# Six experts' weights in three pair slots, and the compressed cache pages spread 5, 7 and 4 a lane over both projections

## The reference

```python
past_cmp = cmp_pool[page_table].reshape(B, PAST_LEN, 2, NSA_KV_HEADS, NSA_HD)
m = kv_rows.astype(F32).reshape(B, L // CMP_BLOCK, CMP_BLOCK, 2, NSA_KV_HEADS, NSA_HD).mean(axis=2)
```

```python
w = jax.nn.softmax(top_l, axis=-1) * grp_w
eid = grp_i * EXPERTS_PER_GROUP + top_i
h = jax.nn.silu(jnp.einsum('nd,edf->nef', x2, w_gate)) * jnp.einsum('nd,edf->nef', x2, w_up)
y = jnp.einsum('nef,efd->nd', h * combine.astype(h.dtype)[..., None], w_down)
```

## Time and profile before

| | |
|---|---|
| median of three runs | 2153.87 us (2149.84 to 2154.89) |
| the profiled execution's own time | 2150.78 us |
| its span | 2149.0 us |
| PE busy | 1638.4 us (76%) |
| DVE busy | 790.3 us (37%) |
| ACT busy | 494.2 us (23%) |
| POOL busy | 181.0 us (8%) |
| queue q1, which carries SP's DMAs | 421.77 MB |
| mean granted clock of PE | 0.857 |

### The profile page before, as it was taken

The page is one execution under the profiler, slowest core; times in us unless marked ns, Lnnn a source line. Parts: engine busy times, 40 slices in busy tenths (PEclk is TensorE's granted clock), DMA queues, the critical chain, the costliest instruction groups (busy, mean ns, idle before and its releaser), DMA issues. The chain is left out here.

```text
span 2149.0 us, 35773 instructions
## 1 busy us (share of the span) xinstructions
PE 1638.4 (76%) x12824; PEld 1195.2 (56%) x12824; DVE 790.3 (37%) x1836; ACT 494.2 (23%) x1250; POOL 181.0 (8%) x282
## 2 busy tenths in 40 slices
PE   4999977888697487775898477875766687487875
PEld 3888866677486244444777355652433376354443
DVE  1666323556302211112155537665544302211112
ACT  2111751222102011111000046773111101111110
POOL 0000003112100311110000000000000000211110
PEclk8999977998597699987799768997787788699997
DMA  3555425200117399992499610006899526299995
GB/s 112 184 173 181 158 79 197 83 5 4 62 59 285 112 426 425 423 407 103 142 313 314 227 63 1 2 2 222 321 343 331 195 69 272 66 424 424 424 422 200
DMA packets 130596, 443.41 MB, mean 206 GB/s; under 512 B 22001, under 2 KB 27634, under 8 KB 112562
## 3 DMA queue, kind: packets, MB, share of 16 engines
q1 hardware_dynamic: 114274, 421.77, 51.7%
q0 software_dynamic: 11008, 17.89, 2.3%
q10 hardware_dynamic: 5200, 2.23, 0.4%
HBM read 426.35 MB, written 43.77 MB: 219 GB/s over the span
## 5 line engine op out<-in xcount | busy, mean ns | idle before, releaser
L1903 PE MATMUL moe_experts_bank_gu<-moe_weights_gu,moe_experts_xT 128*64 128x256 f32 x2048 | 258.4, 416 | 66.5 <-DMA moe_weights_gu<-in_w_gate_up 50.1
L1903 PEld LDWEIGHTS moe_experts_bank_gu<-moe_weights_gu,moe_experts_xT 128*64 128x64 f32 x2048 | 170.6, 151 | 165.8 <-issue 117.5
L408 PE MATMUL proj_acc<-h_gdn,proj_w 128*128 128x272 f32 x1024 | 238.0, 395 | 13.9 <-DMA proj_w<-in_gdn_w 13.9
L408 PEld LDWEIGHTS proj_acc<-h_gdn,proj_w 128*128 128x128 f32 x1024 | 195.8, 191 | 54.9 <-DMA proj_w<-in_gdn_w 14.3
L2143 PE MATMUL nproj_acc<-nsa_h,nproj_w 128*128 128x272 f32 x640 | 151.0, 396 | 11.2 <-DMA nproj_w<-in_nsa_w 11.2
L2143 PEld LDWEIGHTS nproj_acc<-nsa_h,nproj_w 128*128 128x128 f32 x640 | 120.8, 191 | 41.1 <-DMA nproj_w<-in_nsa_w 17.0
L1924 PE MATMUL moe_experts_bank_y<-moe_weights_down,moe_experts_hT 128*64 128x512 f32 x512 | 116.9, 598 | 25.8 <-ACT moe_experts_hT L1953 25.8
L1984 DVE SCALAR_TENSOR_TENSOR moe_experts_h<-moe_experts_bank_gu,moe_table,moe_experts_gate 128x128 f32<-128x128 f32 x64 | 22.5, 351 | 300.0 <-ACT moe_experts_gate L1948 300.0
L282 DVE TENSOR_REDUCE nsa_past_c<-nproj_raw 128x4096 f32 x20 | 88.4, 4420 | 113.2 <-DMA nproj_raw<-in_cmp_pool 113.2
L1656 POOL DMA_INDIRECT table<-moe_router_entry,moe_router_slot_of x20 | 19.2, 962 | 997.1 <-DVE moe_router_place L1614 991.6
L282 DVE TENSOR_REDUCE first_sums<-proj_raw 128x1536 f32 (+1 forms) x32 | 56.1, 1753 | 92.1 <-DMA proj_raw<-in_cmp_pool 92.1
(11 more groups left out here) (487 smaller groups left out, 2582.8 us busy)
## 6 DMA issues: line engine op xcount, KB each, us to landing
moe_weights_gu<-in_w_gate_up SPq DMA_DIRECT2D x64, 2048.0 KB, 20.9
moe_weights_down<-in_w_down SPq DMA_DIRECT2D x64, 1024.0 KB, 22.5
ring_kv<-in_slc_pool SPq DMA_DIRECT2D x256, 256.0 KB, 5.0
nproj_raw<-in_cmp_pool SPq DMA_DIRECT2D x160, 256.0 KB, 4.3
proj_raw<-in_cmp_pool SPq DMA_DIRECT2D x96, 256.0 KB, 2.8
proj_w<-in_gdn_w SPq DMA_DIRECT2D x32, 512.0 KB, 3.2
nproj_w<-in_nsa_w SPq DMA_DIRECT2D x20, 512.0 KB, 5.9
moe_results_y<-y_rows SPq DMA_DIRECT2D x16, 512.0 KB, 6.8
```

The lines of the kernel that those rows point to most:

```text
L408: mm = pe.matmul(acc[s][:, a, 0:HALF], w[s][:, k, :], g.hT[:, k, a * HALF:(a + 1) * HALF], start=(k == 0), stop=(k == KT - 1))
L1903: mm = pe.matmul(gu_bank[m][H, 0:FF], ln.xT[:, k, H], w.gu[:, k, m * FF:(m + 1) * FF], start=(k == 0), stop=(k == KT - 1))
```

## The change

Three things are changed.

*Experts.* `MOE_SLOTS` = 3 pair slots hold the weights of six experts; pair n uses slot n mod 3, while tokens, results and the two lanes stay as they were. `prefetch` loads all six. Thirteen pairs are loaded during the stage, each once the pair three before it has finished with the slot. The loop over pairs is unrolled on all engines, with the pair's number known.

*Room for them.* The expert's h is written over its gate (ACT's silu waits for the turn of h one round before), the norm's squares are written to the buffer that the normed tokens go to, the empty table is the table's own buffer, and the router's row buffers and turned tiles are halves: each token tile is turned, copied and stored as two halves of 512 columns, on buffer 0 and 1. A copy of a tile from 1 on now waits for the same half of the tile before to have landed.

*Pages.* GDN's projection sums 5 pages in each of the 24 convolution tiles and 7 in each of the 8 z tiles, NSA's 4 in each of its 20; `PAGES_EARLY` becomes 176. SP's loop over z tiles is unrolled.

```diff
+MOE_SLOTS = 3
-PAGES_GDN = 3
-PAGES_NSA = 8
-PAGES_EARLY = PAGES_GDN * (CONV_TILES + HEADS)
+PAGES_CONV, PAGES_Z, PAGES_NSA = 5, 7, 4
+PAGES_CONV_END = PAGES_CONV * CONV_TILES
+PAGES_EARLY = PAGES_CONV_END + PAGES_Z * HEADS
...
-        sq = st.sb("sq", [P, KT, TOKENS])
+        sq = g.hT
...
-                with sp.Fori(0, rounds + z_rounds - 1) as i:
+                with sp.Fori(0, rounds) as i:
                     for s in range(2):
...
+                        load_weights(s, i)
+                        pages.load(sp, s, i, (2 * i + s) * PAGES_CONV, PAGES_CONV)
+                for i in range(z_rounds):
+                    for s in range(2):
+                        if i < z_rounds - 1:
+                            load_weights(s, rounds + i)
+                        pages.load(sp, s, rounds + i, PAGES_CONV_END + (2 * i + s) * PAGES_Z, PAGES_Z)
...
-        empty = st.sb("empty", [P, TABLE_COLUMNS, WORDS], U32)
-        rows = [st.sb(f"rows{s}", [P, D_MODEL]) for s in range(2)]
+        empty = g.table
+        rows = [st.sb(f"rows{s}", [P, D_MODEL // 2]) for s in range(2)]
...
+                    for a in range(2):
+                        act.wait_ge(rows_turned, 2 * t + a + 1)
+                        if t >= 1:
+                            act.wait_ge(stored[a], 16 * t)
+                        act.activation(rows[a][0:n, :], turned[a][0:n, :], ACT.Copy).then_inc(rows_out, 1)
...
-            weights = [ExpertWeights(g, st, s, layer) for s in range(2 * MOE_LANES)]
+            weights = [ExpertWeights(g, st, s, layer) for s in range(2 * MOE_SLOTS)]
...
-            ln.h = st.sb(f"h{s}", [P, FF])
+            ln.h = ln.gate
...
-                with eng.Fori(0, rounds) as i:
-                    body(p * rounds + i, i)
+                for pair in range(PAIRS):
+                    body(lanes[pair % MOE_LANES], p * rounds + pair // MOE_LANES, p, pair)
...
-                with sp.Fori(0, rounds - 1) as i:
-                    for ln in lanes:
-                        load(ln, i, i + 1)
+                for pair in range(MOE_SLOTS, PAIRS):
+                    load(pair, (0, pair - MOE_SLOTS))
...
+                            act.wait_ge(ln.pe.sem, ln.pe.past(f"h turned {m}", r - 1))
```

More of the change, by code:

```diff
@@ L1755, in experts_stage @@
             ln.s = s
-            ln.w = weights[2 * s:2 * s + 2]
             ln.x = st.sb(f"x{s}", [P, D_MODEL])
@@ L1777, in over_experts, with weights_of, landed @@
             with eng.Fori(0, passes) as p:
-                with eng.Fori(0, rounds) as i:
-                    body(p * rounds + i, i)
-            return passes
+                for pair in range(PAIRS):
+                    body(lanes[pair % MOE_LANES], p * rounds + pair // MOE_LANES, p, pair)
+            return passes
+        def weights_of(pair):
+            slot = pair % MOE_SLOTS
+            return weights[2 * slot:2 * slot + 2]
+        def landed(p, pair):
+            return 16 * (p * slot_uses(pair % MOE_SLOTS) + pair // MOE_SLOTS + 1)
         def before(ln, r):
@@ L1811, in _ @@
                     with sp.Fori(1, passes) as p:
-                        with sp.Fori(0, rounds) as i:
-                            for ln in lanes:
-                                load(ln, p * rounds + i - 1, i)
+                        for pair in range(PAIRS):
+                            slot = pair % MOE_SLOTS
+                            last_of_slot = slot + MOE_SLOTS * (slot_uses(slot) - 1)
+                            load(pair, (p, pair - MOE_SLOTS) if pair >= MOE_SLOTS else (p - 1, last_of_slot))
             @block.gpsimd
```

244 lines of the change are left out of this document (119 added, 125 removed).

## The result

The changed kernel takes 2158.57 us (median of 20 runs) where the kernel before, in runs between them, takes 2152.2: a ratio of 1.0026, interval 1.0014 to 1.0037. It is slower, by 3 to 8 us, which the 20 runs of each tell from no change. The prediction had 2151, 3 us under the median of before that it started from. The 20 times lie in two bunches, eight from 2153.56 to 2155.9 and twelve from 2158.07 to 2164.14.

What follows compares the result with a forecast made beforehand. It took the experts as bound by DMA, GDN's projection by PE, NSA's by PE and its end by SP. -23.5 + 11 + 10 = -2.5 from the median 2153.87 gave 2151 us, own range 2143 to 2159, whole range 2130 to 2166.

Steps and rivals of the forecast that it cites:

- NSA: NSA's projection with four pages for eight: waits for weights go and its end shortens, -23.5 us (-21 to -26).
- GDN: GDN's projection with five and seven pages for three: z tiles make PE late, +11 us (+7 to +13).
- The tail: End of NSA's projection, last product to next stage: +12.7 us for +25.0, so 12.3 less.
- 1.8 of room: GDN z tile on ACT: the logarithm could wait 1.8 us; a multiplication 6.7 later makes it 4.9 late.
- The hold at the first z tile: GDN, behind the last convolution tile: its taps end later and make the first z product 2.3 us late.
- The tail behind the last product: End of GDN's projection: the seven pages' sum and the multiplications take 11.1 us where 6.7 stood.
- Experts: Third slot: 14.9 us less loading per layer against a router 20 later, +10 us for both layers (+8 to +24).
- the delay: Router: row stores behind the longer preload make PE's counts 20 us later per layer (19 to 27).
- (a): Router: half stores land in 4.6 us, +7 per layer, 2165 us; chance 0.22.
- (b): Experts: the third slot shortens their pace, half the gate-up waits gone gives 2126 us, a quarter 2139; chance 0.22.
- (c): Router: row stores don't stand behind the preload, so it is 4 us later, 2119 us; chance 0.08.
- The unrolled loop: Loop over expert pairs: PE shows no gap between rounds, so unrolling gives nothing.

Runs made afterwards that it cites:

- e6: The changed kernel with the norms' multiplications ahead of the seven-page sum on DVE in a z tile: 2151.65 us, 0.9989 of before.
- e3: The changed kernel with pages at 6 in a convolution tile, 4 in a z tile, 4 in NSA: 2144.42 us, 0.9971 of before.
- e9: The changed kernel with the router reordered as in e4 and pages at 4, 5 and 6: 2112.47 us, 0.981 of before.
- e2: The changed kernel with the pages of before (3, 3 and 8), so the experts' part alone: 2167.16 us, 1.006 of before.
- e5: The changed kernel with two pair slots for three, all else kept: 2158.09 us, 1.0024 of before.
- e8: The changed kernel with the router reordered as in e4 and pages at 6, 4 and 4: 2106.08 us, 0.979 of before.
- after again: A second trace of the changed kernel, nothing changed: span 2150.0 us, for 2162.3 in its first.
- e4: The changed kernel with PE's counts ahead of the turns of tiles 2 to 4, ACT's exponential ahead of tile 1's copies: 2118.28 us, 0.9849 of before.
- e7: The changed kernel with the reorderings of e4 and e6 together: 2112.11 us, 0.9809 of before.

## Why the prediction was wrong, by its own steps

The sum was -23.5 for NSA, +11 for GDN and +10 for the experts, -2.5 together. The first trace of after has -28.0, +17.6 and +13.7 (21.3 - 12.7 + 20.1 - 15.0), together +3.3, and the second -27.7, +18.2 and +13.6, together +4.1; the measured +6.4 has an interval from 3 to 8, and the heads may hold the rest.

- **NSA, mechanism right, 4.5 too small.** The tail was put at -12.3 and is -13.5 (the norms' first product on PE). The products gave 14.5 and not 11.2: besides the waits of the earlier trace rows, the busy time fell from 151.0 to 147.8. It is not the clock, which was 1.00 with the waits too: two products behind a wait took 15.14, 7.57 each, and 20 without a wait take 147.8, 7.39 each. The sum had this at nothing.
- **GDN, the step that failed.** Pages under the convolution tiles cost nothing, the first z tile is held, and the hold recurs at every third tile: all as predicted. The price of a hold was wrong twice. The step from the first multiplication, 6.7 later, to the logarithm with "1.8 of room" let the logarithm follow the multiplication at once, with ACT's table loaded meanwhile; the table load stands behind the same wait, 1.28 us, and the first page came at 3.8 for 3.1. So a hold within the z tiles is 4.28 and 3.54 us and not 2.2. The hold at the first z tile, 2.3 in the sum, is 3.11. And the sum had PE go on at full clock, where 3.79 us for 2.00 add 1.8 to a hold. The three holds are 10.9 us of waiting, 4.0 of longer ones and about 1.1 in one product (8.55 for 7.50), 16.0 for a predicted 6.7. The tail behind the last product is 1.4 longer and not 4.4, since late products gave the last pages time (in e6, without the holds, it is 5.9). e3 and e6 show that the holds within the z tiles come of the seven-page sum ahead of the multiplications, and e3 and e9 that the one at the first z tile comes of the pages of the convolution tiles: 4.50 us behind six, 0.24 behind four.
- **Experts, mechanism and size of the delay right.** The table's landing, predicted at 32 us, is 33.1 and 32.3; the delay, 20 and 20, is 21.3 and 20.1; the experts' gain, 14.9 each, is 12.7 and 15.0. Of the 2.2 us missing in layer 0, 1.7 are one product, the last pair's gate-up, 8.81 us in layer 0 and 7.13 in layer 1:

```profile
999.33 8.81 PE L1921 MATMUL moe_experts_bank_gu<-moe_weights_gu,moe_experts_xT 128*64 128x256 f32 x64 [2.38 <-issue]
...
2117.83 7.13 PE L1921 MATMUL moe_experts_bank_gu<-moe_weights_gu,moe_experts_xT 128*64 128x256 f32 x64 [1.30 <-issue]
```

The granted clock was 0.63 in the first 4.67 us of the first and 1.00 throughout the second. The same product takes 8.81 in e2, e3, e5, e6, e8 and e9, each time behind an idle time of 2.28 to 2.39 us, and 7.13 in after again, e4 and e7, behind 0.6 or less, so that it parts e8 and e9 (-13.1, -12.9) from e4 and e7 (-14.3, -14.5). Why PE is idle for longer ahead of it in some executions was not found.

- **Rivals.** (a), longer landings, didn't come: half rows took a median of 2.1 us from issue to landing, for the 2.25 taken, and the trips 2.7 for 3.0. (b) didn't come: the wait for weights did halve, from 50.1 to 26.0, but the stretch became shorter by the one pair that was no longer loaded, no more. This is what the prediction held against it, that a DMA-bound stage ends with its last byte; no run tested that apart. (c) didn't come: row stores stood behind the preload, 17.49 us of waiting. The Trainium skill ("DMA: Bandwidth & Descriptors", section Queues, rings and completion order) says that each DMA engine takes descriptors in ring order; the table's landing, longer by 15.3 us in layer 0 and 13.4 in layer 1 for 6.29 MB more ahead of it, agrees.
- **The unrolled loop** was put at nothing, and e5 agrees. The rule of the Trainium skill that taken branches cost ("Runtime: NRT & Kernel Launch", section Instruction fetch mechanics) has no effect in this stage that e5 shows.

The sign came out wrong since the sum was a small difference of terms of 10 to 28 us: 6.6 us in GDN and 3.7 in the experts outweighed 4.5 in NSA. The measured 2158.57 lies at the edge of the forecast's own range (2143 to 2159), and that is luck: without the miss in NSA it would be some 4.5 us beyond.

## What to carry to other kernels

A larger preload on the queue that also carries a stage's small stores delays the waits for these stores, here by 13.4 to 15.3 us for 6.29 MB; put the work that doesn't need them ahead in the waiting engines' programs, as e4 does for 40 us, rather than make the preload smaller, which gave nothing in e5. Where a sum is put ahead of work that another engine waits for, follow the wait through that engine's whole program, table loads too, and price PE's hold with the clock that it resumes at. A term that looks like nothing, as the last transfers of a loop, should be looked for again behind the loop once its cover is gone, as e6 shows.
